# Attention on unnormalised exponentials, with the inverse sums turned and applied to the result

## The reference

```
q = (rmsnorm(c_q) @ w_uq)          -> 8 heads of 64 + 32 (rotary)
kv = (rmsnorm(c_kv) @ w_ukv)       -> 8 heads of 64 (keys) + 64 (values)
for each block of 128 queries, each head:
    sc = q_nope @ k_nope.T + q_rope @ k_rope.T
    p = softmax(sc * scale)
    o = p @ v
```

## Time and profile before

| | us |
|---|---|
| median of 3 runs (lowest, highest) | 2642.54 (2639.04, 2643.63) |
| the profiled execution: time, span | 2641.86, 2640.1 |
| query loop of attention, 1383.67 to 1707.07 | 323.4 |
| in it busy: PE, GpSimd, VectorE, ScalarE | 254.94, 237.70, 202.31, 181.99 |

### The profile page before, as it was taken

How to read it: one execution, slowest core, us unless ns; L and a number is a source line. 1 busy time by engine, 2 the same in 40 slices (tenths; PEclk the granted TensorE clock), 3 DMA queues, 4 the chain that set the end, 5 groups by cost and what they waited for, 6 DMA issues and landing times. The chain is left out here.

```text
span 2640.1 us, 26908 instructions
## 1 busy us (share of the span) xinstructions
PE 2347.7 (89%) x10834; PEld 1945.3 (74%) x10834; DVE 1130.1 (43%) x1461; ACT 659.1 (25%) x884; POOL 308.3 (12%) x145
## 2 busy tenths in 40 slices
PE   6999999999978896895957877699799999999997
PEld 5888888888867876785846666577688888888885
DVE  4333333333244394586345666551433333333325
ACT  4211111111022321414225565421321111111112
POOL 1000000000000011110007777500100000000000
PEclk8999999999988998897978999899899999999998
DMA  3211111111021322221330000051221111111101
GB/s 127 80 48 48 46 43 46 48 48 48 16 76 47 89 72 37 64 88 32 120 89 5 6 6 1 31 217 40 64 80 47 44 46 48 48 48 48 48 24 64
DMA packets 174038, 146.95 MB, mean 56 GB/s; under 512 B 27968, under 2 KB 154176, under 8 KB 173952
## 3 DMA queue, kind: packets, MB, share of 16 engines
q1 hardware_dynamic: 173952, 145.77, 18.4%
HBM read 120.58 MB, written 23.07 MB: 54 GB/s over the span
## 5 line engine op out<-in xcount | busy, mean ns | idle before, releaser
L48 PE MATMUL psum<-f_nT_hi,f_w_hi 128*128 128x512 f32 x1408 | 551.6, 392 | 23.9 <-DVE rows L584 23.9
L49 PE MATMUL psum<-f_nT_lo,f_w_hi 128*128 128x512 f32 x1408 | 549.0, 390 | 0.0
L50 PE MATMUL psum<-f_nT_hi,f_w_lo 128*128 128x512 f32 x1408 | 548.4, 390 | 0.0
L48 PEld LDWEIGHTS psum<-f_nT_hi,f_w_hi 128*128 128x128 f32 x1408 | 264.9, 188 | 86.1 <-DVE rows L584 27.8
L584 DVE SCALAR_TENSOR_TENSOR rows<-psum,rows 128x1024 f32<-128x1024 f32 x176 | 215.4, 1224 | 221.2 <-PE psum L50 221.2
L50 PEld LDWEIGHTS psum<-f_nT_hi,f_w_lo 128*128 128x128 f32 x1408 | 264.7, 188 | 55.5
L49 PEld LDWEIGHTS psum<-f_nT_lo,f_w_hi 128*128 128x128 f32 x1408 | 264.9, 188 | 54.3
L48 PE MATMUL psum<-f_d_hi,f_hT_hi 128*128 128x512 f32 x704 | 275.3, 391 | 7.3 <-issue 7.3
L49 PE MATMUL psum<-f_d_lo,f_hT_hi 128*128 128x512 f32 x704 | 275.2, 391 | 0.0
L50 PE MATMUL psum<-f_d_hi,f_hT_lo 128*128 128x512 f32 x704 | 275.1, 391 | 0.0
L532 DVE TENSOR_TENSOR f_w_lo<-f_raw,f_w_hi 128x1024 fp32r<-128x1024 f32 x80 | 97.7, 1221 | 398.2 <-ACT f_w_hi L528 398.2
(11 more groups left out here) (278 smaller groups left out, 3410.1 us busy)
## 6 DMA issues: line engine op xcount, KB each, us to landing
f_raw<-ffn_w_gate SPq DMA_DIRECT2D x44, 512.0 KB, 4.8
f_raw<-ffn_w_up SPq DMA_DIRECT2D x44, 512.0 KB, 3.8
f_raw<-ffn_w_down SPq DMA_DIRECT2D x44, 512.0 KB, 3.5
g_raw<-w_in SPq DMA_DIRECT2D x16, 512.0 KB, 4.6
gates<-rows SPq DMA_DIRECT2D x10, 512.0 KB, 3.0
rows<-x SPq DMA_DIRECT2D x8, 512.0 KB, 7.9
kept<-rows SPq DMA_DIRECT2D x1, 4096.0 KB, 12.8
gl_gate<-gates SPq DMA_DIRECT2D x8, 512.0 KB, 4.8
```

The lines of the kernel that those rows point to most:

```text
L48: pe.matmul(out, lhs_hi, rhs_hi, start=first, stop=False)
L49: pe.matmul(out, lhs_hi, rhs_lo, start=False, stop=False)
L50: return pe.matmul(out, lhs_lo, rhs_hi, start=False, stop=last)
```

## The change

The exponentials are no longer multiplied. They are turned as they are; the sums of four blocks (tot, now a column for each) are inverted in one instruction that writes each inverse 64 times (inv, 128 x 256), PE turns that into rows 0 to 63 of bank 7 (`inverses`), and VectorE multiplies the group's result by it. So att is now made by two instructions, `sum` and the product, and a projection that goes into bank 7 next waits for the product (`av`). The turned tiles have two halves of 128 x 512 (PARTS = 2), each with a turning, a cast and a subtraction of its own, and the scores stand between the two turnings on PE. LAG goes from 3 to 2, prob keeps three slots (SLOTS_P), the projections move to blocks 0, 1, 4, 5 and the queries to 2, 3. On ScalarE the exponential moves to the head of the next step, and a projection is read in the step in which it is made.

```diff
-        KD, HALF_R, LAG = NOPE + ROPE, ROPE // 2, 3
-        PROJECT_AT, QUERIES_AT = (1, 2, 5, 6), (3, 4)
+        KD, HALF_R, LAG, SLOTS_P, PARTS = NOPE + ROPE, ROPE // 2, 2, 3, 2
+        PROJECT_AT, QUERIES_AT = (0, 1, 4, 5), (2, 3)
...
+        tot = sb("tot", [P, 2, 4])
+        inv = sb("inv", [P, 2, 4, VH])
+        spread, total = sb("spread", [VH, HALF]), sb("total", [VH, HALF])
...
+        inv_out = psum[0:VH, 7, :]
...
                     pe.wait_ge(s["proj_act"], job)
                     pe.wait_ge(s["proj_dve"], job)
+                    if n >= 2 and x in (0, 2):
+                        pe.wait_ge(s["av"], 2 * n - 3 + x // 2)
...
+            def inverses(J):
+
+                pe.wait_ge(s["inv"], J + 1)
+                pe.wait_ge(s["proj_act"], min(2 * JOBS + 2 * J, HEADS * JOBS))
+                pe.wait_ge(s["proj_dve"], min(2 * JOBS + 2 * J, HEADS * JOBS))
+                for i in range(4):
+                    t = pe.transpose(inv_out[:, i * P:(i + 1) * P], inv[:, J % 2, i, :], ident[:])
+                t.then_inc(s["inv_t"], 1)
...
             for g in range(G + LAG + 2):
+                turning = LAG <= g < G + LAG
+                if turning:
+                    turn(g - LAG, 0)
                 if g < G:
                     scores(g)
-                if LAG <= g < G + LAG:
-                    turn(g - LAG)
+                if turning and PARTS == 2:
+                    turn(g - LAG, 1)
                 if values_after(g):
                     values(*values_after(g))
+                    if values_after(g)[1] == 1:
+                        inverses(values_after(g)[0])
...
-            def inverse(g):
-                sl = g % LAG
-                dve.wait_ge(s["exp"], g + 1)
-                if g >= LAG:
-                    dve.wait_ge(s["norm"], g - LAG + 1)
-                dve.reciprocal(inv[:, sl:sl + 1], tot[:, sl:sl + 1]).then_inc(s["inv"], 1)
+            def inverse(J):
+
+                dve.wait_ge(s["exp"], 4 * J + 4)
+                if J >= 2:
+                    dve.wait_ge(s["inv_t"], J - 1)
+                dve.reciprocal(inv[:, J % 2], tot[:, J % 2].unsqueeze(2).broadcast_to([P, 4, VH])).then_inc(s["inv"], 1)
...
                 dve.wait_ge(s["spread"], J + 1)
+                dve.tensor_tensor(total[:], pv_out[0:VH], spread[:], ALU.add).then_inc(s["sum"], 1)
+                dve.wait_ge(s["inv_t"], J + 1)
                 if J >= 2:
                     dve.wait_ge(s["av_lo"], J - 1)
-                dve.tensor_tensor(att[rows, J % 2, :], pv_out[0:VH], spread[:], ALU.add).then_inc(s["av"], 1)
+                dve.wait_ge(s["sum"], J + 1)
+                dve.tensor_tensor(att[rows, J % 2, :], inv_out, total[:], ALU.mult).then_inc(s["av"], 1)
...
-            def normalized(g):
-                sl = g % LAG
-                pool.wait_ge(s["inv"], g + 1)
-                pool.tensor_scalar(prob[:, sl, :], prob[:, sl, :], inv[:, sl:sl + 1], None, ALU.mult).then_inc(s["norm"], 1)
```

More of the change, by code:

```diff
@@ L1422, in attention_phase @@
         rot = sb("rot", [P, 2, HALF])
-        prob = sb("prob", [P, LAG, SEQ])
+        prob = sb("prob", [P, SLOTS_P, SEQ])
         PT_lo = sb("PT_lo", [P, 3, ST, 2 * P], F32R)
-        nmx, tot, inv = (sb(n, [P, LAG]) for n in ("nmx", "tot", "inv"))
-        spread = sb("spread", [VH, HALF])
-        att = sb("att", [P, 2, HALF])
+        nmx = sb("nmx", [P, SLOTS_P])
+        tot = sb("tot", [P, 2, 4])
+        inv = sb("inv", [P, 2, 4, VH])
+        spread, total = sb("spread", [VH, HALF]), sb("total", [VH, HALF])
+        att = at("att", [P, 2, HALF], F32, 24 * KB)
         names = ("trig wv_in wv_hi wv_lo lt l_hi l_lo rot0 kr kr_hi kr_lo v_mm v_hi v_lo raw_in w_hi w_lo proj proj_act proj_dve rot q_sum q_hi q_lo "
-                 "scores nmx exp inv norm tr tr_hi tr_lo pv spread av av_hi av_lo").split()
+                 "scores nmx exp inv inv_t tr tr_hi tr_lo pv spread sum av av_hi av_lo").split()
         s = {n: sem(n) for n in names}
@@ L1438, in attention_phase @@
         JOBS = 4
[L1439 removed]
+        KP = ST // PARTS
+        turned_bank = lambda x: psum[:, 4:6, :].rearrange("p b (k q) -> p (b k) q", q=P)[:, x * KP:(x + 1) * KP, :]
         pv_out = psum[:, 6, :]
@@ L1529, in scores, with turn @@
                 mm.then_inc(s["scores"], 1)
-            def turn(g):
-                pe.wait_ge(s["norm"], g + 1)
+            def turn(g, x):
+                if x == 0:
+                    pe.wait_ge(s["exp"], g + 1)
                 if g == 0:
@@ L1615, in spread_out @@
                 if J:
-                    act.wait_ge(s["av"], J)
+                    act.wait_ge(s["sum"], J)
                 act.copy(spread[:], pv_out[VH:2 * VH]).then_inc(s["spread"], 1)
@@ L1728, in _ @@
                 h, qt = g // ST, g % ST
-                if 1 <= g <= G:
-                    inverse(g - 1)
+                if g >= 5 and g % 4 == 1 and g // 4 - 1 < NB:
+                    inverse(g // 4 - 1)
+                if LAG <= g < G + LAG:
+                    turned(g - LAG, 0)
+                if g < G:
+                    maximum(g)
+                if LAG <= g < G + LAG and PARTS == 2:
+                    turned(g - LAG, 1)
                 if g and values_after(g - 1) and values_after(g - 1)[1] == 1:
                     attended(values_after(g - 1)[0])
-                if g and g - 1 < G and job_after(g - 1):
-                    project(*job_after(g - 1))
-                if g < G:
-                    maximum(g)
-                if LAG <= g < G + LAG:
-                    turned(g - LAG)
+                if g < G and job_after(g):
+                    project(*job_after(g))
                 if qt == 7 and h + 2 < HEADS:
@@ L1743, in _, with queries @@
         def _(pool):
-            def queries(n, x, before):
-                if before:
-                    pool.wait_ge(s["norm"], before)
-                elif x:
-                    pool.wait_ge(s["q_lo"], x)
+            def queries(n, x):
+                if n * 2 + x:
+                    pool.wait_ge(s["q_lo"], n * 2 + x)
+                if n and x == 0:
+                    pool.wait_ge(s["av_lo"], attended_by(n))
                 pool.wait_ge(s["rot"], n * 2 + x + 1)
@@ L1754, in queries, with attended_by, attended @@
                 pool.tensor_tensor(QT_lo[0:KD, n % 2, hs(x)], qf[0:KD, x, :], QT_hi[0:KD, n % 2, hs(x)].bitcast(F32), ALU.subtract).then_inc(s["q_lo"], 1)
-            def normalized(g):
-                sl = g % LAG
-                pool.wait_ge(s["inv"], g + 1)
-                pool.tensor_scalar(prob[:, sl, :], prob[:, sl, :], inv[:, sl:sl + 1], None, ALU.mult).then_inc(s["norm"], 1)
-            def attended(J, normed, asked):
+            def attended_by(n):
+                at = (n - 1) * ST + QUERIES_AT[0]
+                return sum(1 for g in range(at) if values_after(g) and values_after(g)[1] == 1)
+            def attended(J, asked):
                 h = J // 2
                 rows = slice(h % 2 * VH, (h % 2 + 1) * VH)
-                if h % 2:
-                    pool.wait_ge(s["norm"], normed)
-                    pool.wait_ge(s["q_lo"], asked)
+                pool.wait_ge(s["q_lo"], asked)
+                if J:
+                    pool.wait_ge(s["av_lo"], J)
                 pool.wait_ge(s["av_hi"], J + 1)
```

67 lines of the change are left out of this document (33 added, 34 removed).

## The result

| | before | after |
|---|---|---|
| median of 5 runs (lowest, highest), us | 2642.03 (2639.04, 2643.63) | 2651.99 (2649.60, 2653.07) |
| span of the profiled execution, us | 2640.1 | 2647.8 |

The account below looks back on a forecast made before the run. A chain of handovers was taken to bound the loop; first head 33.4, middle heads 235.2, last head 30.3 and tail 18.5 gave 317.4 us against 323.4, 6 us less: 2636.5 us, range 2620 to 2655.

Parts of the forecast that it names:

- What bounded the kernel: Attention query loop, 323.4 us: a chain of handovers, with GpSimd's multiplication doing harm twice a head; other six steps short.
- The ring: ScalarE and VectorE, once a block: half eviction, half subtraction, maximum to exponential, next ScalarE instruction; step floor of 3.58 us.
- the bank's wait: PE's projections in blocks 0 and 4 wait for the product before using bank 7: about 3 us, 12 times.
- the long steps: Steps at blocks 0 and 4 of a middle head, maximum to maximum: 9.3 and 7.7 us.
- The reciprocal: VectorE's 128 x 256 reciprocal, queued ahead of the half subtraction in long steps: 1.77 us, bounds 0.46 and 2.2.
- Rival 3: VectorE's wide reciprocal is cheap, at its lower bound; long steps of 8.3 and 7.0 us: 2624 us, chance 0.12.
- rival 4: VectorE's wide reciprocal costs 8.3 ns a column, 5 us more over 14 places: 2641.5 us, no change; chance 0.13.
- The bank doesn't hold PE: Every head is PE's own load of 31.0 us, the loop falls a further 49: 2587 us, chance 0.07.
- the sum of the middle heads: Six middle heads of 39.2 us each, against 39.1 before: 235.2 us, with nothing added for a lower PE clock.
- rival 5: PE's clock falls in the new waits, costing 1.8 to 5.8 us a head: slower, 2650 us, chance 0.23.
- the last head: No projections, but exp stands behind the aT_hi cast: 6.0 us twice, plus 11.1 and 7.1, in all 30.3.
- the tail: From the last maximum to the loop's end: PE starts values at 9.1, they take 5.3; in all 18.5 us.

Follow-up runs that it names:

- e4_no_scaling: Kernel before the change, without the multiplication of the exponentials, the small reciprocals and the waits for them: 2598.49 us, 0.9824 of before.
- e7_fill_narrow: Changed kernel with useless matmuls filling PE's waits for the product, and a 4-column reciprocal plus repeating copy for the wide one: 2634.01 us, 0.9960 of before.
- e12_and_narrow: Changed kernel with projections a block later and ahead of values, aT_hi cast a step later, 4-column reciprocal plus repeating copy: 2597.78 us, 0.9821 of before.
- e1_fill: Changed kernel with 12 useless matmuls in each of PE's 12 waits for the product ahead of a projection: 2643.18 us, 0.9992 of before.
- e9_again: Changed kernel run and profiled once more, with no edit: 2651.81 us, 1.0028 of before.
- e5_late: Changed kernel with projections a block later, their reading on ScalarE and VectorE and the aT_hi cast a step later too: 2670.96 us, 1.0104 of before.
- e2_shift: Changed kernel with projections at blocks 1, 2, 5, 6 and queries at 3, 4: 2633.03 us, 0.9953 of before.
- e10_projection_first: Changed kernel with projections at blocks 1, 2, 5, 6, made on PE ahead of that step's values: 2636.49 us, 0.9975 of before.
- e11_and_cast_later: Changed kernel with projections a block later and ahead of values, and ScalarE's cast of aT_hi a step later: 2620.96 us, 0.9918 of before.

## Why the prediction was off

- **What bounded the kernel**: right in the main. Without the multiplications the old order is 46 us shorter (e4_no_scaling). That the other six steps of a head were already short is too simple: a middle head before has steps of about 4.2, 5.5, 4.5, 5.3, 8.3, 4.2, 3.6 and 3.3 us.
- **The ring, the bank's wait, the long steps**: right in mechanism and size: 3.57 for 3.58; 12 waits of 3.0 us; 9.52 and 7.76 for 9.3 and 7.7; a head at full clock 39.2 for 39.2. Of the 0.2 that the long step is over the sum, the gap from sum to product is 0.07 (0.78, 0.71 taken); the rest lies in the handovers.
- **The reciprocal**: 1.735 us for 1.77. Rival 3 (cheap) and rival 4 (8.3 ns a column) fall; (1735 - 157) / 255 is 6.2 ns a column. At block 0 it ended last, as summed; at block 4 ScalarE's side ends as late, which the sum had 0.7 shorter (rival 3's 8.3 and 7.0 with a cheap reciprocal are 8.3 to 8.6 and 7.5 to 7.8 in e7_fill_narrow).
- **The bank doesn't hold PE** (rival 2): false for this change, no middle head came near 31. With the waits arranged away e12_and_narrow comes to 33.4.
- **The step that failed is the clock**: the sum of the middle heads holds PE at full clock behind the waits for the bank and puts the cost of a fall at nothing, with rival 5 left beside it at 0.23 because "the idle share of PE does not grow, which speaks against". That was wrong evidence: PE's idle share did not grow, but behind waits of 3 us the clock fell to 0.50 in four heads of six. The six heads take 243.7 us in place of 235.2. e1_fill shows the cause: PE at work in the same stretches, the clock at 1.00 and the heads at 39.2 again; and in e9_again the long heads are others.
- **The other mis-sized terms**: the last head (33.9 us for 30.3) and the tail (20.1 for 18.5), 5.2 us together. The last head has clock 0.85 and steps of 4.41, 4.56 and 5.25 where the sum had 3.6 to 4.65. In the last of these, which begins at 1689.8, PE is busy without a gap and at half clock at first:

```profile
1689.00:1691.00 2.00, 2.00 (x8) 1.60 (x8) 1.74 (x2) 0.32 (x1) 0.00 (x0) 0.50 0.00 0
1691.00:1693.00 2.00, 2.00 (x8) 1.57 (x7) 0.74 (x2) 1.37 (x3) 0.00 (x0) 0.73 0.00 0
```

So the clock is the likely cause here too, but that is argued from windows: no edit held it up in this head (e1_fill, which fills no wait there, has 35.1 us for it). In the tail PE's values begin 10.1 us behind the last maximum (9.1 predicted), and take 5.8 us for 5.3.
- **The sum of it**: 8.5 + 5.2 us, less 0.4 in the first part, are the 13.4 between 317.4 and 330.8 within rounding, and 13.4 less the forecast gain of 6 is the loss of 7.4 us in the loop. The clock in the middle heads alone would have given 325.9 us, 2.5 over the 323.4 of before: no change, by the prediction's own measure. It costs 1.4 us a head, less than the 1.8 to 5.8 of rival 5 and than the 1.9 from which that rival was to decide. That the time (2652) lies so near rival 5's 2650 is therefore in part luck; the last head and the tail made up what the middle heads had less.
- **Where there was something to win**: at full clock a middle head takes 39.2 us, and it took 39.1 before. The gain lay in the first part (39.1 to 33.0) and in the tail (23.6 to 20.1); the last head has no wait for GpSimd to lose and grew from 26.1 to 33.9. Of that the sum had 4.2: the two steps with the cast of aT_hi ahead of the exponential (6.09, 4.24 before) and the ring of 3.57, where the old order with LAG 3 has steps of 3.05. What the ring would be with LAG 3 in the new order was not tried.

My expectations on the way failed where I left out who else uses bank 7 (e5_late), what stands behind a late projection (e2_shift), that a projection ahead of the values leaves PE no slack for the values and inverses behind them, and that the clock falls there (both e10_projection_first).

## What to carry to other kernels

Taking work from an engine that others wait for pays only as far as no new wait is put in the same place: list, for each wait that a change adds, which instructions stand behind it on that engine, and place the producer of a shared bank and its readers so that one step lies between. Do not judge PE's clock by its idle share: here the share shrank and the clock fell. Look at the granted clock in the windows behind each wait, price the matmuls there at the low clock too, and take a second profile, since the heads it strikes change. Where several waits are stacked on one ring, an edit tried alone may show a fraction of its worth (4 to 7 us of 23 here), so try the edits together before dropping one. And look at every part of a loop for what there is to win: the last head had no wait to remove, and lost 8 us.

## What the runs showed of the hardware

- The same wait of 2.95 to 2.97 us on PE was followed by the full clock in some heads and by 0.50 in others, and in another execution of the same kernel in other heads. In e11_and_cast_later 0.50 followed waits of only 0.68 and 1.33 us, one soon after the other.
- A reciprocal on VectorE costs 157 ns for one column, 163 for four, 353 for 32 and 1735 for 256.
- A VectorE copy of 128x256 float32 within SBUF takes 293 ns by itself and up to 1336 when a GpSimd instruction runs as it begins; the wide reciprocal was never lengthened (1733 to 1753), though in the changed kernel one begins at 1443.55, beside a GpSimd instruction from 1443.53 to 1444.81.
